# Eight head pairs rolled into a loop, with the first scores of a pair stacked and a no-op ahead of TensorE's batches

## The reference

```python
def rwkv7_scan(r, w, k, v, kk, a):
    def step(state, inp):
        r_t, w_t, k_t, v_t, kk_t, a_t = inp
        sa = jnp.einsum('bhvk,bhk->bhv', state, -kk_t)
        state = (state * w_t[:, :, None, :] + sa[..., None] * (kk_t * a_t)[:, :, None, :]
                 + v_t[..., None] * k_t[:, :, None, :])
        return state, jnp.einsum('bhvk,bhk->bhv', state, r_t)
...
for d in range(2):
    ...
    o = rwkv7_scan(*ins)          # d == 1: on the flipped sequence
    bonus = jnp.sum(rh * kd * r_k, axis=-1, keepdims=True) * vh
    dir_out.append((group_norm(o, gn_w, gn_b) + bonus.reshape(nB, S, D)) * g)
y = dir_out[0] + dir_out[1]
```

## Time and profile before

| what | value |
|---|---|
| median of three runs | 2549.98 us |
| the three runs | 2556.03, 2549.98, 2548.55 us |
| profiled execution, its own time | 2556.03 us |
| its span in the profile | 2554.1 us |
| TensorE busy | 2398.3 us, 94% of the span |
| VectorE, ScalarE, GpSimd busy | 46%, 35%, 29% |
| mean granted TensorE clock | 0.981 |

### The profile page before, as it was taken

The page is one execution under the profiler, slowest core; times in us unless marked ns, Lnnn a source line. Parts: engine busy times, 40 slices in busy tenths (PEclk is TensorE's granted clock), DMA queues, the critical chain, the costliest instruction groups (busy, mean ns, idle before and its releaser), DMA issues.

```text
span 2554.1 us, 49960 instructions
## 1 busy us (share of the span) xinstructions
PE 2398.3 (94%) x21476; PEld 1684.4 (66%) x21476; DVE 1185.4 (46%) x1957; ACT 897.5 (35%) x1598; POOL 739.0 (29%) x431
## 2 busy tenths in 40 slices
PE   7999899999889999998889998999997999999998
PEld 5876678887634467777777844888875766743443
DVE  6047242031153665556565514396304899726011
ACT  4257333233122344344444323355323222361011
POOL 3310234344200044333344202444432433420101
PEclk9999999999999999999999999999998999999999
DMA  4311122222212100000000011244222333222222
GB/s 144 106 61 59 66 75 91 99 94 87 89 42 82 66 16 10 10 9 10 9 3 10 23 55 50 99 164 153 86 90 81 110 111 112 91 76 73 83 66 74
DMA packets 49897, 181.01 MB, mean 71 GB/s; under 512 B 5600, under 2 KB 5856, under 8 KB 49440
## 3 DMA queue, kind: packets, MB, share of 16 engines
q1 hardware_dynamic: 46064, 166.95, 19.4%
q10 hardware_dynamic: 3632, 11.08, 1.1%
HBM read 167.45 MB, written 10.55 MB: 70 GB/s over the span
## 4 chain that ended last, share of the span: by engine, by line
PE 81%; issue 9%; DVE 5%; ACT 4%; POOL 1%; DMA 0%; POOLq 0%; ACTq 0%; DVEq 0%
PE ps L559 15%; PE ps L556 14%; PE ps L557 13%; PE ps L558 13%; PE ps L817 5%; PE ps L780 3%; PE ps L599 2%; PE ps L797 1%; PE ps L734 1%; PE ps L1001 1%; PE ps L808 1%; PE ps L646 1%; PE ps L934 1%; POOL ring_lo L2028 1%; PE ps L661 1%
## 5 line engine op out<-in xcount | busy, mean ns | idle before, releaser
L2028 POOL TENSOR_TENSOR ring_lo<-ring,ring_hi 128x1024 fp32r<-128x1024 f32 x198 | 482.7, 2446 | 897.9 <-ACT ring_hi L1052 897.7
L559 PE MATMUL ps<-arena,ring 128*128 128x512 f32 x1024 | 452.3, 599 | 20.6 <-DVE arena L1755 11.7
L558 PE MATMUL ps<-u_lo,ring_hi 128*128 128x512 f32 x968 | 385.3, 398 | 0.0
L559 PEld LDWEIGHTS ps<-arena,ring 128*128 128x128 f32 x1024 | 194.7, 192 | 274.0 <-issue 239.7
L1052 ACT ACTIVATE ring_hi<-ring 128x1024 fp32r<-128x1024 f32 x198 | 207.1, 1051 | 78.8 <-DMA ring<-in_wall 75.1
L556 PE MATMUL ps<-mlp_u_hi,ring_hi 128*128 128x512 f32 x512 | 212.4, 415 | 8.8 <-POOL ring_lo L2028 7.4
L558 PEld LDWEIGHTS ps<-u_lo,ring_hi 128*128 128x128 f32 x968 | 184.3, 190 | 43.6
L556 PE MATMUL ps<-mid_hi,ring_hi 128*128 128x512 f32 x512 | 208.2, 407 | 0.0
L557 PE MATMUL ps<-mlp_u_hi,ring_lo 128*128 128x512 f32 x512 | 204.3, 399 | 0.0
L558 PE MATMUL ps<-mid_lo,ring_hi 128*128 128x512 f32 x512 | 202.5, 395 | 0.0
L557 PE MATMUL ps<-mid_hi,ring_lo 128*128 128x512 f32 x512 | 202.4, 395 | 0.0
(11 more groups left out here) (392 smaller groups left out, 3981.3 us busy)
## 6 DMA issues: line engine op xcount, KB each, us to landing
ring<-in_wall SPq DMA_DIRECT2D x273, 512.0 KB, 3.4
s_tables<-arena ACTq DMA_DIRECT2D x16, 512.0 KB, 3.1
arena<-s_tables SPq DMA_DIRECT2D x16, 512.0 KB, 3.7
arena<-bias_lines SPq DMA_DIRECT2D x16, 448.0 KB, 4.4
arena<-in_lora SPq DMA_DIRECT2D x8, 384.0 KB, 3.0
h<-in_x SPq DMA_DIRECT2D x1, 2048.0 KB, 7.7
out<-arena ACTq DMA_DIRECT2D x8, 256.0 KB, 2.9
consts<-in_consts SPq DMA_DIRECT2D x1, 1280.0 KB, 13.7
```

The costliest lines, as they stand in the source:

```text
L558: return nc.tensor.matmul(y, w_hi, low, start=False, stop=x == k - 1)
L559: return nc.tensor.matmul(y, ring[:, at:at + P], rhs(x), start=x == 0, stop=x == k - 1)
L2028: G.tensor_tensor(ring_lo[:, slot], ring[:, slot], ring_hi[:, slot].bitcast(F32), ALU.subtract).then_inc(sem("weights_split"), 1)
```

## The change

- `over_pairs` runs pair 0, then a hardware loop of 3 rounds with two pairs each (pairs 1 to 6), then pair 7. In the loop each count and address is a register's value.
- The scores' A and C batches become one `each_stacked` per direction into A and C. So A and C each hold one head's ka.al and be.al. Semaphore counts change from 11 to 9 per pair.
- VectorE takes T and Ma out of these banks by two half-partition multiplications each (`halves`). TT is one multiplication. The units are added afterwards: T's on GpSimd at the start of the pair, TT's on VectorE. GpSimd's `units` copies are gone.
- X of level 1 waits for Ma (`masked_v`), because X overwrites bank A; before, `each_half` waited for it.
- `out_gated` moves from level 4 to behind level 5's updates.
- A no-op that isn't merged away stands ahead of TensorE's batches, and ahead of two groups of GpSimd's instructions, so the last wait sits on it and not on the first product.

```diff
-        def over_pairs(body):
-
-            def of_pair(i):
-                return (lambda per, c=0: i * per + c) if 0 <= i < DT else None
-
-            for i in range(DT):
-                body(i % 2, of_pair(i), of_pair(i - 1), of_pair(i + 1))
+        def over_pairs(engine, body):
+            def fixed(i):
+                return lambda per, c=0: i * per + c
+
+            body(0, fixed(0), None, fixed(1))
+            with engine.Fori(0, (DT - 2) // 2) as r:
+                for q in range(2):
+                    prev, n, nxt = [lambda per, c=0, k=k: r * (2 * per) + (k * per + c) for k in (q, q + 1, q + 2)]
+                    body(1 - q, n, prev, nxt)
+            body((DT - 1) % 2, fixed(DT - 1), fixed(DT - 2), None)
...
             def each(out, a, b):
+                pe.nop(nofuse=True)
...                                  # the same in each_turned, each_crossed, each_stacked, each_half
-                    each_crossed(A[d], F[d]["be"], F[d]["al"]).then_inc(sem("scores_ready"), 1)
+                    each_stacked([A[d], C[d]], F[d], F[d]["al"]).then_inc(sem("scores_ready"), 1)
                 pe.wait_ge(sem("z_taken"), n(6, 6))
                 for d in range(2):
                     each_crossed(B[d], F[d]["al"], F[d]["be"]).then_inc(sem("scores_ready"), 1)
-                for d in range(2):
-                    each(C[d], F[d]["ka"], F[d]["al"]).then_inc(sem("scores_ready"), 1)
...
                         if l == 1:
                             pe.wait_ge(sem("t_started"), n(2, d + 1))
+                            pe.wait_ge(sem("masked_v"), n(6, d + 1))
...
                         if l == 1:
                             pe.wait_ge(sem("tt_started"), n(2, d + 1))
-                            pe.wait_ge(sem("masked_v"), n(6, d + 1))
...
                             pe.wait_ge(sem("state_ready"), n(14, k - 1))
+                        pe.nop(nofuse=True)
...
                         pe.wait_ge(sem("w_taken"), n(16, k + 1))
+                        pe.nop(nofuse=True)
...
                         pe.wait_ge(sem("u_taken_too"), n(16, k + 1))
+                        pe.nop(nofuse=True)
...
-                def placed(name, b, kind, i):
-                    return V_.copy_predicated(chunks(R[d][name]), mask(kind, i).bitcast(mybir.dt.int32), chunks(bank(4 * d + b)))
+                def halves(d, name, kind, crossed):
+                    for e in range(2):
+                        half = 1 - e if crossed else e
+                        ins = TT(chunks(of_head(R[d][name], half)), chunks(of_head(bank(4 * d + 2 * e), half)),
+                                 of_head(mask(kind, d), half), ALU.mult)
+                    return ins
                 for d in range(2):
-                    dve.wait_ge(sem("scores_ready"), n(11, 1 + d))
-                    dve.wait_ge(sem("t_filled"), n(2, d + 1))
-                    placed("T", 0, "level_n", d).then_inc(sem("t_started"), 1)
+                    dve.wait_ge(sem("scores_ready"), n(9, 1 + d))
+                    halves(d, "T", "level_n", True).then_inc(sem("n_masked"), 1)
                 for d in range(2):
                     dve.wait_ge(sem("l_copied"), n(2, d + 1))
-                    dve.wait_ge(sem("tt_filled"), n(2, d + 1))
-                    placed("TT", 1, "level", d * LEVELS).then_inc(sem("tt_started"), 1)
+                    TT(chunks(R[d]["TT"]), chunks(bank(4 * d + 1)), mask("level", d * LEVELS), ALU.mult
+                       ).then_inc(sem("tt_masked"), 1)
                 for d in range(2):
-                    dve.wait_ge(sem("scores_ready"), n(11, 5 + d))
-                    TT(chunks(R[d]["Ma"]), chunks(bank(4 * d + 2)), mask("strict", d), ALU.mult).then_inc(sem("masked_v"), 1)
+                    halves(d, "Ma", "strict", False).then_inc(sem("masked_v"), 1)
+                eye = const("eye", 0, CH).unsqueeze(1).to_broadcast([P, NCH, CH])
+                for d in range(2):
+                    dve.wait_ge(sem("tt_masked"), n(2, d + 1))
+                    TT(chunks(R[d]["TT"]), chunks(R[d]["TT"]), eye, ALU.add).then_inc(sem("tt_started"), 1)
...
                             dve.wait_ge(sem("with_bonus"), prev(2, 2))
-                            out_gated(prev, G)
                         if nxt:
                             features(nxt, G, p_end[1 - parity], 2)
+                    if l == 5 and prev:
+                        out_gated(prev, G)
...
+                for d in range(2):
+                    pool.wait_ge(sem("n_masked"), n(2, d + 1))
+                    G.tensor_tensor(chunks(R[d]["T"]), chunks(R[d]["T"]), eye, ALU.add).then_inc(sem("t_started"), 1)
                 for d in range(2):
                     pool.wait_ge(sem("l_copied"), n(2, d + 1))
                     level_mask(1, d)
...
-            for name in ("TT", "T"):
-                for d in range(2):
-                    units(name, d)
-            over_pairs(pair)
+            over_pairs(pool, pair)
```

More of the change, by code:

```diff
@@ L956, in pair @@
                         hidden_product(nxt, 2, j - 4, 1)
-            over_pairs(pair)
+            over_pairs(pe, pair)
             out_variances(last)
@@ L1364, in pair @@
                 for d in range(2):
-                    act.wait_ge(sem("scores_ready"), n(11, 3 + d))
+                    act.wait_ge(sem("scores_ready"), n(9, 3 + d))
                     taken(R[d]["L"], bank(4 * d + 1), "l_copied")
@@ L1382, in pair @@
                     if l == 5:
-                        act.wait_ge(sem("scores_ready"), n(11, 11))
+                        act.wait_ge(sem("scores_ready"), n(9, 9))
                         for e in range(2):
@@ L1409, in pair @@
                     nc.scalar.activation(dev[d], o_sb[d], ACT.Square).then_inc(sem("o_squared"), 1)
-            over_pairs(pair)
+            over_pairs(act, pair)
             out_logs(last)
@@ L1860, in pair @@
                         for d in range(2):
-                            dve.wait_ge(sem("scores_ready"), n(11, 7 + d))
+                            dve.wait_ge(sem("scores_ready"), n(9, 5 + d))
                             for name, b in (("M0", 0), ("M1", 3)):
@@ L1908, in _ @@
                 features(first, feats[0], p_end[0], step)
-            over_pairs(pair)
+            over_pairs(dve, pair)
             out_scaled(last, feats[(DT - 1) % 2])
@@ L2057, in features @@
                         pool.wait_ge(sem("kd_factor"), n(2, d + 1))
+                        pool.nop(nofuse=True)
                         G.tensor_tensor(r["kd"], r["kd"], pair_tile(kTr, n), ALU.mult).then_inc(sem("kd_ready"), 1)
@@ L2066, in features @@
                         G.tensor_tensor(r["ka"], r["ka"], r["kd"], ALU.mult).then_inc(sem("features_p"), 1)
-            def units(name, d):
-                eye = const("eye", 0, CH).unsqueeze(1).to_broadcast([P, NCH, CH])
-                G.tensor_copy(chunks(R[d][name]), eye).then_inc(sem("t_filled" if name == "T" else "tt_filled"), 1)
             def pair(parity, n, prev, nxt):
@@ L2085, in pair @@
                 if nxt:
-                    features(nxt, feats[1 - parity], 0)
-                    for d in range(2):
-                        pool.wait_ge(sem("dt_ready"), n(10, 9 + d))
-                        units("TT", d)
-                    features(nxt, feats[1 - parity], 1)
-                    pool.wait_ge(sem("scores_ready"), n(11, 11))
+                    for step in range(2):
+                        features(nxt, feats[1 - parity], step)
+                    pool.wait_ge(sem("scores_ready"), n(9, 9))
+                    pool.nop(nofuse=True)
                     stage_v(nxt)
-                    for d in range(2):
-                        pool.wait_ge(sem("u_ready"), n(16, 15 + d))
-                        units("T", d)
             first = lambda per, c=0: c
```

3 lines of the change are left out of this document (2 added, 1 removed).

## The result

The changed kernel takes 2616.22 us (median of four runs, 2615.22 to 2616.85), the kernel before 2549.27 (2548.49 to 2556.03): ratio 1.0256, 95% interval 1.0239 to 1.0274. It is 67 us slower. The forecast was 2582, 32 us slower, and its range ended at 2607: the direction was right, and the size was under half of what came.

What follows compares the result with a forecast made beforehand. The prediction took TensorE to be the bound, busy in 94% of the span, its code arriving one block per some 3.86 us. Terms 0 + 7.5 + 7.4 + 12.8 + 4 = 31.7 on 2549.98 gave 2582 us; range 2560 to 2607.

Steps and rivals of the forecast that it cites:

- place of `out_gated`: Behind level 5, VectorE's first u copies queue behind it: 1.05 us in seven pairs, +7.4 us, bounds 0 and 15.
- loop: back edges, its register operations and code: Two backward branches wait for code, 6.4 us each (+12.8); exposed register operations in the recurrence +1.0; added level code.
- part of 4: Levels 3 to 5: no-ops and register operations add instructions where code already arrives late, +4 us, bounds 0 and 8.
- no-ops in the recurrence and levels: A separate wait lengthens hops in 64 recurrence rounds, 6.5 us; in the levels, added instructions share the 4 us.
- scores to level 1: At each pair's start: scores end some 1.8 us sooner on TensorE, but this becomes a wait for VectorE; taken as 0.
- the rival of a cheap branch: At the loop's back edges: the branch doesn't wait for code, or other waits cover it; 2569 us, chance 0.17.
- a second late block: Behind each back edge: the pair's dense first code waits for another instruction block, about 2.5 us net.
- the rival of all register operations exposed: In looped pairs: TensorE's sequencer doesn't run ahead, so every register operation costs time, 24 us; 2606 us, chance 0.17.
- two hops of 51 ns: Recurrence rounds: no-ops taking the waits lengthen the hops to u's product and the state product, 6.5 us over 64 rounds.
- Rival 3: Scores to level 1: the shorter scores come through, -14.4 us; 2537 with the other terms at low bounds, chance 0.06.
- Rival 4: Whole kernel: extra waits mostly fall in idle time and the scores' gain pays the rest; 2550 us, chance 0.08.
- a microsecond later: Sign in each first recurrence round: VectorE's first u copy starts a microsecond after its release.

Runs made afterwards that it cites:

- gated_back: The changed kernel with `out_gated` back in level 4, nothing else: 2585.42 us, ratio 1.0131.
- gated_unrolled: The changed kernel with `out_gated` in level 4 and the pairs written out instead of the hardware loop: 2567.2 us, ratio 1.007.
- nops_only: The kernel before with only the no-ops ahead of TensorE's batches added: 2559.03 us, ratio 1.0035.
- scores_only: The kernel before with only the new scores, halves and units; pairs written out, no no-ops, `out_gated` in level 4: 2560.72 us, ratio 1.0043.
- behind_one_filler: The changed kernel; GpSimd's next features wait for `out_gated`, and one unused TensorE product precedes the looped first rounds' u wait: 2595.58 us, ratio 1.0181.
- fillers: The changed kernel with three unused 128x512 TensorE products ahead of the looped pairs' first-round wait for u: 2604.08 us, ratio 1.0209.
- gated_hint: gated_back with a prefetch hint for the loop's backward branch at the head of each engine's loop body: 2584.75 us, ratio 1.013.
- whole_masks: scores_only with each pair of half-partition masks as one 128-partition operation, some values then not the reference's: 2547.96 us, ratio 0.9988.
- features_behind: The changed kernel, but GpSimd starts the next pair's features only when `out_gated` is done: 2604.44 us, ratio 1.0202.

## Why the prediction was wrong

| term | forecast | measured | from |
|---|---|---|---|
| place of `out_gated` | +7.4 | +30.8 | after less gated_back |
| loop: back edges, its register operations and code | +12.8, 1.0, part of 4 | +18.2 | gated_back less gated_unrolled |
| no-ops in the recurrence and levels | +6.5, part of 4 | +9 | nops_only |
| scores to level 1 | 0 | +11 | scores_only |
| sum | +31.7 | +67 | of which the last two make only 18 together |

**`out_gated`, the step that failed.** The forecast's mechanism was right as far as it went: it queues ahead of the first u copies and the ring waits. Two further costs were missing. The term took 2.14 us from the earlier trace rows, where the operations run without GpSimd beside them, and carried them to a place where GpSimd is at work. It said of GpSimd only that its earlier start "is worth nothing". The overlap doesn't hang on that earlier start: already in the kernel before, GpSimd's features run from 1251.15 on, across the new place, which the earlier trace rows have at 1254.32:

```profile
1253.84 1.25 POOL L2058 TENSOR_TENSOR arena<-arena 128x512 f32<-128x512 f32 x1
1255.07 1.26 POOL L2059 TENSOR_TENSOR arena<-arena 128x512 f32<-128x512 f32 x1
```

Whether the 2.1 us by which they start sooner add to the cost wasn't tested. Per looped pair: the bare shift is 1.05 us (first rounds 4.50 to 4.61 in behind_one_filler against 3.53), just the forecast's figure. GpSimd's share is about 2.3 (fillers, where the clock holds: 6.74 to 7.07). The clock's is another 1.5 (8.20 to 8.60). Together some 4.8 x 6 and 1.0 in the last pair, 30. Against gated_back's own seven first rounds, three of which are at half clock too, it is 26. Even the forecast's high bound, 15, was half the 30.8 measured. Rows of the kernel before, in its timeline of level 2 of the fifth pair, had the price of the overlap:

```profile
1228.84 3.42 POOL L2074 TENSOR_TENSOR ring<-ring,consts 128x512 f32<-128x512 f32 x2 [3.09 <-PE ps L780]
1229.37 1.76 DVE L1857 SCALAR_TENSOR_TENSOR u<-u,cols,arena 128x512 f32<-128x512 f32 x1
```

The same kind of operation as `out_gated`'s takes 1.76 us beside GpSimd, and GpSimd's two take 3.42 us where the earlier trace rows have 2.51. The price and the neighbour both stood in the trace before and weren't read. The price of the clock stood there too: three of the first rounds there last 4.8 to 5.3 us instead of 3.53.

**The backward branches.** Right in kind, and the rival of a cheap branch (2569) is refuted: 3.38 and 3.88 us, beside a forecast of 3.86 for the first block. The other 2.5 us of the forecast were to be a second late block. What came instead is TensorE's half clock, which lengthens the scores behind an edge by 1.1. That makes some 5 us an edge (3.5 and 4.0 of idle, 1.1 each): 9.7 for both against a forecast of 12.8. gated_hint shows by the branch's time that it waited for code; the Trainium skill ("Runtime: NRT & Kernel Launch", "Instruction fetch mechanics") has this as a forced fetch behind a taken branch, and the trace now agrees at 3.4 to 3.9 us. Some 8.5 of the loop's 18.2 us are left. The levels can hold them: their sum over all pairs is 321.2 us in gated_back and 312.9 in gated_unrolled. But the profiled executions of these two lie 25.9 us apart and not 18.2. They also differ by 7.7 us of idle at the edges, by 2.3 in the scores, and by 4.6 in the first two rounds of each pair, where the clock is low in four pairs of the one and in one of the other. So the split of the 18.2 stays open. Whether register operations or the code that they add make the levels longer wasn't tested; the rival of all register operations exposed (24 us) is larger than the whole loop.

**Recurrence.** Quiet rounds last 2.34 us unrolled, as forecast, and 2.37 to 2.52 in the loop. But nearly all of the 0.10 lies in one hop, from the w copy to VectorE's u copy (0.09); the state product had its separate instruction already. The forecast's two hops of 51 ns gave the right length of a round by the wrong split, which is luck.

**Scores to level 1.** That the saving on TensorE turns into a wait for VectorE was right, and whole_masks shows it; the full price of halves was right too (0.70). The half product was put at 9.4 and came at 10.3 in the fifth pair (10.4 on the mean in scores_only), because the units' addition, taken at its free 0.64, meets GpSimd's masks and takes up to 1.76. It is the same omission as in `out_gated`. Rival 3 (faster) is refuted: without the halves 3 us are to be had, not 14. Rival 4 (no change) is refuted by the result.

**The other rivals.** The profile's signs named ahead came as said: 3.5 and 4.0 us of idle at the two back edges, rounds of 2.34 to 2.4, X released by VectorE. Only "a microsecond later" for VectorE's first u copy came as 2.9 to 3.5 us behind ScalarE's in the looped pairs; in features_behind it is 1.0 to 1.1, the bare shift again. Apart from this, the three first rounds at half clock (and a second one) made the profiled execution of the kernel before 5.9 us longer. It lay 6.1 above the median that the forecast set out from; with only one execution profiled, it is not shown that the one explains the other.

## What to carry to other kernels

When an operation moves, take its duration from the conditions of its new place: look in the timeline at what the other engines do there. An idle time on TensorE can have a second price behind it, in the work done before its clock returns; here it was some 1.5 us in a first round, more than the 1.05 of the bare shift. The trace of before can hold the price: look for the same kind of operation where it takes longer than usual, and for what runs beside it there. And where the same stretch of a kernel lasts 3.53 us in one pair and 5.06 in another, find out why before work is moved next to it.

## What the runs showed of the hardware

- A VectorE operation of 0.69 to 0.75 us with its inputs in SBUF took 1.53 to 1.75 us where it began second beside GpSimd's tensor operations, and ended 0.54 to 0.55 us after them. Where it began first it kept 0.75, and GpSimd's took 1.72 instead of 1.26. With GpSimd held back it was at 0.75 and 0.69 in all pairs.
- TensorE's clock fell to 0.50 inside an idle stretch of 3.1 us, and inside one of 1.2 to 1.3 in four looped pairs of six (features_behind). In the kernel before it fell in three first rounds whose idle stretches were the same 0.3 to 0.4 us as in those where it held. One product of 128x512 in the gap (1.13 us for its two records) left all six looped first rounds at 4.5 to 4.6 us at full clock.
- A taken branch over some 7,000 instructions cost TensorE 3.4 to 3.9 us, the other engines' 40 to 67 ns. A hint brought it to 0.37 to 0.40, and a stop of 2.8 us appeared where the loop ends.
- VectorE's multiplications out of PSUM took 2.81 us for four on 64 partitions (0.69 for one) and 0.69 for one on 128.
